# Feed-forward quarters 2 and 3 in 512-column passes, up and down alternating; two vector jobs of the narrow block placed later

## The reference, cut to what matters

```python
hdn = modulate(rmsnorm(x, norm2_g[l]), shift2, scale2)          # 256 x 1024
ff = jnp.square(jax.nn.relu(hdn @ w_ff1[l])) @ w_ff2[l]         # 1024 -> 4096 -> 1024
x = x + gate2[:, None, :] * ff
```

```python
out = jnp.concatenate([o_f, o_att, o_c, o_p], axis=-1) @ w_out  # o_c: the convolution branch
x_new = x + gate[:, None] * out
```

## Time and profile before

| | us |
|---|---|
| median of 3 runs (1375.07 to 1375.34) | 1375.18 |
| the profiled execution, its own time | 1374.65 |
| its span, from the first to the last instruction | 1372.5 |
| PE busy in it | 1329.8 |
| DVE busy | 942.5 |
| ACT busy | 737.4 |

### The profile page before, as it was taken

The page is one execution under the profiler, slowest core; times in us unless marked ns, Lnnn a source line. Parts: engine busy times, 40 slices in busy tenths (PEclk is TensorE's granted clock), DMA queues, the critical chain, the costliest instruction groups (busy, mean ns, idle before and its releaser), DMA issues.

```text
span 1372.5 us, 24612 instructions
## 1 busy us (share of the span) xinstructions
PE 1329.8 (97%) x10268; PEld 1218.2 (89%) x10268; DVE 942.5 (69%) x1367; ACT 737.4 (54%) x1203; POOL 60.5 (4%) x49
## 2 busy tenths in 40 slices
PE   6999999999999999999999999999999999998998
PEld 3998899998999998998999998999997778687987
DVE  3877976667688876478755566978575656538673
ACT  3565475564645534555666555544554555426562
POOL 0010000201000001010000210000100000011000
PEclk9999999999999999999999999999999999999999
DMA  9974555677799995744744467976552122132430
GB/s 345 356 237 166 168 209 180 211 255 240 234 323 374 357 372 181 228 132 132 275 154 128 150 218 261 318 244 220 177 167 92 62 93 81 43 101 73 144 123 31
DMA packets 194721, 269.51 MB, mean 196 GB/s; under 512 B 5037, under 2 KB 174386, under 8 KB 188338
## 3 DMA queue, kind: packets, MB, share of 16 engines
q1 hardware_dynamic: 194610, 267.94, 57.8%
HBM read 266.87 MB, written 1.05 MB: 195 GB/s over the span
## 4 chain that ended last, share of the span: by engine, by line
PE 78%; DVE 12%; ACT 5%; issue 3%; SPq 1%; DMA 1%; DVEq 0%; ACTq 0%
PE first_dense L1758 13%; PE first_dense L1762 12%; PE first_dense L1760 12%; PE first_dense L1075 5%; PE first_dense L1078 5%; PE first_dense L1077 5%; DVE first_w_lo L560 3%; PE first_s L1758 2%; PE first_s L1762 2%; PE first_s L1760 2%; PE first_dense L1937 2%; ACT first_w_hi L554 1%; PE first_o L1762 1%; PE first_t L1762 1%; PE first_t L1760 1%
## 5 line engine op out<-in xcount | busy, mean ns | idle before, releaser
L560 DVE TENSOR_TENSOR first_w_lo<-first_raw,first_w_hi 128x1024 fp32r<-128x1024 f32 (+2 forms) x304 | 366.5, 1219 | 185.0 <-ACT first_w_hi L554 182.9
L554 ACT ACTIVATE first_w_hi<-first_raw 128x1024 fp32r<-128x1024 f32 (+2 forms) x304 | 313.5, 1041 | 232.2 <-PE first_dense L1762 90.6
L1758 PE MATMUL first_dense<-first_h_parts,first_w_hi 128*128 128x256 f32 x1312 | 374.5, 285 | 3.0 <-DVE first_h_parts L2392 1.7
L1760 PE MATMUL first_dense<-first_h_parts,first_w_hi 128*128 128x256 f32 x1312 | 371.1, 283 | 0.0
L1762 PE MATMUL first_dense<-first_h_parts,first_w_lo 128*128 128x256 f32 x1312 | 371.0, 283 | 0.0
L1758 PEld LDWEIGHTS first_dense<-first_h_parts,first_w_hi 128*128 128x128 f32 x1312 | 251.5, 192 | 12.4 <-issue 8.1
L1760 PEld LDWEIGHTS first_dense<-first_h_parts,first_w_hi 128*128 128x128 f32 x1312 | 251.6, 192 | 0.0
L1762 PEld LDWEIGHTS first_dense<-first_h_parts,first_w_lo 128*128 128x128 f32 x1312 | 251.6, 192 | 0.0
L1077 PE MATMUL first_dense<-first_parts,first_w_hi 128*128 128x512 f32 (+1 forms) x400 | 137.0, 342 | 0.0
L1075 PE MATMUL first_dense<-first_h_parts,first_w_hi 128*128 128x512 f32 (+1 forms) x336 | 118.4, 352 | 1.4 <-DVE first_w_lo L731 0.9
L1078 PE MATMUL first_dense<-first_h_parts,first_w_lo 128*128 128x512 f32 (+1 forms) x336 | 115.6, 344 | 0.0
(11 more groups left out here) (418 smaller groups left out, 2624.4 us busy)
## 6 DMA issues: line engine op xcount, KB each, us to landing
first_raw<-in_w_in SPq DMA_DIRECT2D x78, 1024.0 KB, 5.3
first_raw<-in_w_ff SPq DMA_DIRECT2D x64, 1024.0 KB, 7.9
first_units<-in_w_ada SPq DMA_DIRECT2D x34, 1024.0 KB, 6.6
first_units<-in_w_mod SPq DMA_DIRECT2D x17, 1024.0 KB, 6.8
first_raw<-in_w_out SPq DMA_DIRECT2D x16, 1024.0 KB, 5.3
first_mb<-in_w_ada SPq DMA_DIRECT2D x10, 1024.0 KB, 7.9
first_mb<-in_w_mod SPq DMA_DIRECT2D x7, 1024.0 KB, 7.3
first_raw<-in_w_uq SPq DMA_DIRECT2D x6, 768.0 KB, 4.4
```

Of the source, the lines that this page charges most:

```text
L554: act.activation(w_hi[g % SPLIT][:, c], raw[g % CHUNK_RING][:, c], ACT.Copy).then_inc(hi_made, 1)
L560: dve.tensor_tensor(w_lo[g % SPLIT][:, c], raw[g % CHUNK_RING][:, c], w_hi[g % SPLIT][:, c].bitcast(F32), ALU.subtract).then_inc(lo_made, 1)
L1758: pe.matmul(out, still[0](t), moving[0](t), start=start and t == n == 0, stop=False, skip_group_check=True)
L1760: pe.matmul(out, still[0](t), moving[1](t), start=False, stop=False, skip_group_check=True)
```

## The change

The up steps of quarters 1 and 2 become wide. A wide step takes both banks. For each weight tile and half it sends the high and the low part of the activations through the high weight together, as one matmul of 512 columns, and adds the low weight's product with one of 256 columns: 16 of each in place of 48 of 256. ACT then copies the second half of each bank away, DVE adds the first half to it and so frees the bank, ACT does the Relu in place and both squares, and DVE makes the low part of the activations one step later. Up and down steps of these quarters alternate: steps 4 to 11 are up 1 and down 0 in turns, steps 12 to 19 up 2 and down 1. The folds and row products keep their step numbers.

```diff
-FF_ORDER = [("up", 0), ("up", 1), ("down", 0), ("up", 2), ("down", 1), ("up", 3), ("down", 2), ("down", 3)]
-FF_STEPS = [(kind, q, c) for kind, q in FF_ORDER for c in range(4)]
+FF_ORDER = [[("up", 0)], [("up", 1), ("down", 0)], [("up", 2), ("down", 1)], [("up", 3)], [("down", 2)], [("down", 3)]]
+FF_STEPS = [(kind, q, c) for kinds in FF_ORDER for c in range(4) for kind, q in kinds]
...
+def is_wide(j):
+    return j >= FF and FF_STEPS[j - FF][0:2] in (("up", 1), ("up", 2))
...
-    return 2 if is_out(j) else 1
+    return 2 if is_out(j) or is_wide(j) else 1
```

PE, and ACT:

```diff
+                def wide_up(j):
+                    w = [view(part[(base + j) % SPLIT], j) for part in (w_hi, w_lo)]
+                    banks = [bank_of(RING[base + j] + c) for c in range(2)]
+                    for t in range(KT):
+                        if 2 * t in (0, KT):
+                            pe.wait_ge(lo_made, 2 * (base + j) + 1 + (t > 0))
+                        for c in range(2):
+                            f = slice(c * P, (c + 1) * P)
+                            pe.matmul(two(banks[c]), w[0][:, t, f], h_parts[:, :, t, :], start=t == 0, stop=False,
+                                      skip_group_check=True)
+                            last = pe.matmul(banks[c][:, 0:S], w[1][:, t, f], h_hi[:, t, :], start=False,
+                                             stop=t == KT - 1, skip_group_check=True)
...
+                def up_squares(j):
+                    n, (_, q, c) = UP_NO[j], FF_STEPS[j - FF]
+                    if n >= 2:
+                        reach(act, ff_ready, n - 1)
+                    act.activation(relu_sq[n % 2], relu[n % 2], ACT.Square)
+                    if c == 0 and q >= 2:
+                        act.wait_ge(unit_done, DONE[base + DOWN_END[q - 2]])
+                    act.activation(ff_hi[q % 2][:, 2 * c:2 * c + 2, :], relu[n % 2],
+                                   ACT.Square).then_inc(ff_hi_made.sem, 1)
...
+                    if is_wide(j):
+                        r, u = relu[UP_NO[j] % 2], RING[base + j]
+                        for e in range(2):
+                            act.wait_ge(unit_done, DONE[base + j] + e + 1)
+                            act.activation(r[:, e, :], dense[(u + e) % 2][:, S:2 * S], ACT.Copy).then_inc(part_moved.sem, 1)
+                        for e in range(2):
+                            wait_evacuated(act, u + e)
+                        link(act.activation(r, r, ACT.Relu))
+                        up_squares(j)
+                        return
```

DVE:

```diff
+                def up_low(j):
+                    n, (_, q, c) = UP_NO[j], FF_STEPS[j - FF]
+                    reach(dve, ff_hi_made, n + 1)
+                    dve.tensor_tensor(ff_lo[q % 2][:, 2 * c:2 * c + 2, :], relu_sq[n % 2],
+                                      ff_hi[q % 2][:, 2 * c:2 * c + 2, :].bitcast(F32),
+                                      ALU.subtract).then_inc(ff_ready.sem, 1)
...
+                    elif is_wide(j):
+                        r, u = relu[UP_NO[j] % 2], RING[base + j]
+                        for e in range(2):
+                            reach(dve, part_moved, 2 * WIDE_NO[j] + e + 1)
+                            dve.tensor_tensor(r[:, e, :], r[:, e, :], dense[(u + e) % 2][:, 0:S],
+                                              ALU.add).then_inc(evacuated[(u + e) % 2], 1)
                     elif j in UP_NO:
+                        up_low(j)
+                    elif is_down(j) and is_wide(j - 1):
+                        up_low(j - 1)
```

In the second block the low part of the second half of the narrow layer's second chunk moves from the end of the wide layer's DVE part to behind `x_tiles` of the narrow one, and the two splits of the convolution's result move one unit on, into `fourier_seq`:

```diff
-            conv_lag = 1 if ctx_out else 2
+            conv_lag = 1 if ctx_out else 3
...
                     x_tiles()
+                    split_low2(dve, *behind(0, N_CHUNKS2 - 1, SPLIT), 1)
                     newton(dve, link, t_bank[1][:, 0:S], ctx_rstd, D, EPS, (squared.sem, squared.left + 2), (ssq2_used.sem, ssq2_used.left + 2))
...
-                    if new:
+                    if new and not (ctx_out and out_pair(n) == 3):
                         split_low2(dve, *new, 1)
```

More of the change, by code:

```diff
@@ L162 @@
 UP_NO = {FF + i: 4 * q + c for i, (kind, q, c) in enumerate(FF_STEPS) if kind == "up"}
+WIDE_NO = {j: n for n, j in enumerate(j for j in UP_NO if is_wide(j))}
 DOWN_END = {q: FF + i + 1 for i, (kind, q, c) in enumerate(FF_STEPS) if kind == "down" and c == 3}
@@ L211 @@
                     prob_ready=24, arg_ready=8, arg_exp=8, prob_t_ready=24, o_hi_made=12, o_ready=12,
-                    gate_ready=12, merge_added=8, merged_hi=4, merged_ready=4, ff_hi_made=16, ff_ready=16,
+                    gate_ready=12, merge_added=8, merged_hi=4, merged_ready=4, ff_hi_made=16, ff_ready=16, part_moved=2 * len(WIDE_NO),
                     x_ready=4)
@@ L1739, in layer @@
                 Counted(first_sems[n], FIRST_COUNTS[n] * l) for n in ("gate_ready", "merge_added", "merged_hi", "merged_ready"))
-            ff_hi_made, ff_ready, x_ready = (Counted(first_sems[n], FIRST_COUNTS[n] * l) for n in ("ff_hi_made", "ff_ready", "x_ready"))
+            ff_hi_made, ff_ready, part_moved, x_ready = (Counted(first_sems[n], FIRST_COUNTS[n] * l)
+                                                for n in ("ff_hi_made", "ff_ready", "part_moved", "x_ready"))
             def norm_added(norm):
@@ L1923, in by_features @@
                     return products(j, outs, nk, **options)
+                def wide_up(j):
[10 more added lines that the diff above has]
+                                             stop=t == KT - 1, skip_group_check=True)
+                            if t == KT - 1:
+                                last.then_inc(unit_done, 1)
+                        if 2 * t + 2 == KT:
+                            last.then_inc(half_used, 1)
                 def lead(j, chunks):
@@ L1987, in chunk @@
                                         (o_hi[branch], o_lo[branch]), 4, frees=e == 1).then_inc(unit_done, 1)
+                    elif is_wide(j):
+                        wide_up(j)
                     elif is_down(j):
@@ L2138, in evacuate @@
                         else:
-                            n, (_, q, c) = UP_NO[j], FF_STEPS[j - FF]
+                            n = UP_NO[j]
                             act.activation(relu[n % 2], two, ACT.Relu).then_inc(done, 1)
                             wait_evacuated(act, u)
-                            if n >= 2:
-                                reach(act, ff_ready, n - 1)
-                            act.activation(relu_sq[n % 2], relu[n % 2], ACT.Square)
-                            if c == 0 and q >= 2:
-                                act.wait_ge(unit_done, DONE[base + DOWN_END[q - 2]])
-                            act.activation(ff_hi[q % 2][:, 2 * c:2 * c + 2, :], relu[n % 2],
-                                           ACT.Square).then_inc(ff_hi_made.sem, 1)
+                            up_squares(j)
                 if l:
@@ L2375, in evacuate @@
                         residual(2 * (j - WOUT), dense[u % 2], 16, j == FF - 1).then_inc(evacuated[u % 2], 1)
-                    elif j in UP_NO:
-                        n, (_, q, c) = UP_NO[j], FF_STEPS[j - FF]
-                        reach(dve, ff_hi_made, n + 1)
-                        dve.tensor_tensor(ff_lo[q % 2][:, 2 * c:2 * c + 2, :], relu_sq[n % 2],
-                                          ff_hi[q % 2][:, 2 * c:2 * c + 2, :].bitcast(F32),
-                                          ALU.subtract).then_inc(ff_ready.sem, 1)
+                    elif is_wide(j):
+                        r, u = relu[UP_NO[j] % 2], RING[base + j]
[3 more added lines that the diff above has]
+                                              ALU.add).then_inc(evacuated[(u + e) % 2], 1)
+                    elif j in UP_NO:
+                        up_low(j)
+                    elif is_down(j) and is_wide(j - 1):
+                        up_low(j - 1)
                     elif is_down(j) and FF_STEPS[j - FF][1] == 3:
```

## The result

The changed kernel takes 1411.24 us (median of 4 runs, 1410.73 to 1412.4), the kernel before 1375.26 beside it: a ratio of 1.0258, 95% interval 1.0245 to 1.0271. The forecast was 1406, the range 1388 to 1420. The profiled execution took 1412.4 us with a span of 1410.6.

The account below looks back on a forecast made before the run. PE led with DVE close behind; DVE was to become the bound wherever every step has a fold. Terms 12.8 + 14.7 + 4.5 + 0.1 - 1.0 = +31.1 on 1374.65 gave 1405.8, median 1406 us, range 1388 to 1420.

Parts of the forecast that it names:

- DVE's forced idle time, 2.83 us in each wide step: In wide steps DVE idles from its addition until ACT has done Relu, squares and high part: 2.83 us, bounds 2.7 to 3.1.
- A pair of steps costs DVE 13.3 us: A wide step (8.1) and the down step behind it (5.15) cost DVE 13.3 us; PE needs 11.3.
- PE feels it at the row products, 6, 6 and 7 us ahead of steps 12, 20 and 12 of layer 1: PE idles for late folds at row products: some 6 us before steps 12, 20 of layer 0, 7 before 12 of layer 1.
- Layer 0, 12.8 us up to step 20; layer 1, 14.7 up to step 22: Feed-forward stages: DVE's lag through late folds loses 12.8 us in layer 0 and 14.7 us in layer 1.
- The clock, 4.5 us: After three long PE stalls the granted clock falls, losing 1.5 us each, 4.5 us in all, bounds 0 and 8.
- The whole: Whole kernel: 12.8 + 14.7 + 4.5 + 0.1 - 1.0 = +31.1 us, 1406 us, 2.3% slower.
- PE's gain, 3.4 us in 16 wide steps: Matmuls of 512 columns replacing pairs of 256 save PE 0.21 us per wide step, 3.4 us if nothing else moves.
- The convolution's splits, 1.0 us: Narrow layer: splits moved behind DVE's sums of `fourier_seq` shorten PE's wait, gaining 1.0 us, between 0.3 and 1.2.
- The moved low part, 0.1 us of loss: Narrow layer: low part moved behind `x_tiles` brings x 1.05 us earlier but leaves PE's restart unchanged; +0.1 us taken.
- Nothing for banks and weights: Feed-forward: bank waits taken as costing nothing; late weights in layer 0 cost 0 to 2 us, inside DVE's own bounds.

Follow-up runs that it names:

- act_order: Changed kernel, but in a wide step ACT makes the high part of the next weights' second half before waiting for DVE's additions: 1372.76 us, 0.9976 to the kernel before.
- fold_first: Changed kernel, but in a wide step DVE does its folds between the additions and the second low part: 1373.11 us, 0.9976 to the kernel before.
- awake: Changed kernel plus 48 unused 256-column matmuls on PE before the fold waits at steps 12, 20 (layer 0) and 12, 22 (layer 1): 1406.13 us, 1.0215.
- one_quarter: Changed kernel with only the second quarter's up steps wide (8 wide steps, not 16), all orders kept: 1395.61 us, 1.0141 to the kernel before.
- order_only: Kernel before with only the alternating up and down steps of the second and third quarter, no 512-column passes: 1377.24 us, 1.0006.
- both_orders: Changed kernel with ACT's high part moved ahead of its wait and DVE's folds moved before the second low part: 1372.82 us, 0.9974 to the kernel before.
- only_conv: Kernel before with only the narrow layer's convolution high and low parts one stage later: 1375.22 us, 0.9990.
- only_low: Kernel before with only the low part of the first narrow layer's last weights' second half moved behind x_tiles: 1376.11 us, 0.9999.
- wide_only: Changed kernel with the old order, four wide steps then four down steps, activations' low part at the next step's head: 1411.02 us, 1.0253 to the kernel before.
- wide_three: Changed kernel with ACT's high part and DVE's folds both moved earlier, plus the fourth quarter's up steps wide, 24 wide steps: 1377.09 us, 1.0009 to the kernel before.
- small_folds: Changed kernel with the modulation weights' folds cut from 2048 (or 1024) to 8 columns, all waits kept: 1369.38 us, 0.9949 to the kernel before.

## Why the prediction was right, step by step

- *DVE's forced idle time, 2.83 us in each wide step.* Right. It is 2.88 to 2.90 in all 16 wide steps, released by the high part on ACT. With the idle time taken away on either engine (act_order, fold_first) the loss goes as a whole. This was shown, not only argued.
- *A pair of steps costs DVE 13.3 us.* Right, 13.31. The two additions need 0.33 from start to start, as taken.
- *PE feels it at the row products, 6, 6 and 7 us ahead of steps 12, 20 and 12 of layer 1.* Right: 6.09, 6.09, 6.71, and 3.69 ahead of step 22.
- *Layer 0, 12.8 us up to step 20; layer 1, 14.7 up to step 22.* Measured 6.2 + 9.8 = 16.0 and 9.7 + 6.5 = 16.3, in each of which one stretch at half clock is contained. awake puts it at 2.0 in layer 0 and 1.6 in layer 1. That leaves 14.0 and 14.7, together 28.7 where I had 27.5: layer 1 as forecast, layer 0 1.2 more, for which I have no reason. one_quarter bears the 2.0 out: its 12->20 is 49.96, that of order_only, which has the same order and 256 columns, 47.92. In layer 1 it has 62.44 against 59.70, 2.7 and not 1.6; PE sets the pace there behind the wait, where in the change DVE does again, which may be why.
- *The clock, 4.5 us.* The mis-sized term. There were four stalls with a loss of clock, not three (I had worked out the wait at step 22 but given it none), and in the change they cost 2.0, 2.5, 1.6 and 2.5 us, not 1.5 each: behind the first of them the windows have 0.50 for 4 us and 0.84 for 4 more, where the earlier trace rows, which I had taken, has 0.59 for 4. Together 8.6 us, 4.1 more than forecast and just above my upper bound of 8. awake shows the cause, with 5.9 us less by the ratios, net of the delay that it adds itself.
- *The whole.* The profiled execution's span grew by 38.1 us, the sum had 31.1. The clock gives 4.1 of the missing 7.0, layer 0's lag 1.2, the opening 1.1, small pieces around the narrow layer the rest. The main ones have the same sign, so the forecast isn't near by errors that cancel. The lower end of the range doesn't follow from its terms: 1406 - 3 - 4.5 - 0.5 - 5 is 1393, not 1388. The measured 1411.24 is far from it.
- *PE's gain, 3.4 us in 16 wide steps.* Too large. both_orders has 0.61 to 0.64 us less in each of the four stretches with four wide steps, 0.16 a step and 2.5 in all. In the change itself none of it was to be seen, since DVE set the pace. The Trainium skill (TensorE: Matmul & The Clock Gate, section "Wait — 56ns, not 53.3ns?") with its 2.5 ns per matmul gave an estimate of 0.6, the rows gave 3.4; the runs lie between, nearer to the rows.
- *The convolution's splits, 1.0 us.* Right: 1.62 to 0.59 of idle time, and 1.05 in only_conv.
- *The moved low part, 0.1 us of loss.* The mechanism is right: x and the lead come 1.0 earlier, and at PE's restart it is given back. The 0.15 of only_low is too small to be told from the spread. In the change the clock fell while PE did the matmuls ahead of the restart (0.57 from 1296 to 1300 us), so it had no wait in front of it; it came 23.42 us behind the first sum, near the others.
- *Nothing for banks and weights.* Right in this order of the steps, since a down step needs no bank. It was the order that made it so: with wide steps in a row PE pays at the banks (24.3 us in wide_only, of which about half is DVE's lag and half the hand-over of 1.0 us a step that wide_three shows; the halves are an estimate, 12 x 1.0 of 24.3).

## What to carry to other kernels

When a step is split so that one engine hands half-done data to another and waits for it back, look at what stands behind the returning wait on both engines: here one unrelated instruction behind it on ACT made the difference between 1.0258 and 0.9976. An engine that is busy for 90% of a stage's time has no room for a wait of 2.9 us in every second step, even if its share of the kernel is 69%. Where a bound engine makes the matmul engine wait in long pieces, count the clock on top, for each piece: here 1.6 to 2.7 us behind waits of 3.7 to 6.7 us. And a step that fills both banks leaves the next such step nothing to write to, so put a step with another bank between them.

## What the runs showed that I had not expected

A pair of 512 and 256 columns doesn't always take the same time. Timeline of PE, the first and the last of the sixteen 512-column matmuls in two wide steps of small_folds, 5.22 and 5.30 us apart:

```profile
370.84 0.40 PE L1942 MATMUL first_dense<-first_h_parts,first_w_hi 128*128 128x512 f32 x1
...
376.06 0.39 PE L1942 MATMUL first_dense<-first_h_parts,first_w_hi 128*128 128x512 f32 x1
...
382.15 0.40 PE L1942 MATMUL first_dense<-first_h_parts,first_w_hi 128*128 128x512 f32 x1
...
387.45 0.40 PE L1942 MATMUL first_dense<-first_h_parts,first_w_hi 128*128 128x512 f32 x1
```

In some wide steps the pairs are 0.347 apart throughout, in others they go 0.361, 0.349, 0.350 in turn, 0.353 on the mean; in act_order the two kinds of step alternate strictly, in all 16. Three matmuls of 256 columns take 0.360. This is why the gain is 0.16 a step and not 0.21. No run tells why; banks, buffers and shapes are the same in both kinds, and it stays open.
